# A diffusion layer in split fp32: the up projection by 512-column matmuls, with GpSimd off the weight splits

## The reference

```python
def conv_glu_ffn(h, w_up, conv_w, w_down, grid):
    up = h @ w_up                      # (256, 2048) @ (2048, 11264)
    up = dwconv2d_grid(up, conv_w)     # 3x3 taps per channel over a 4 x 64 grid
    a, b = jnp.split(up, 2, axis=-1)   # D_FF = 5632 each
    return (jax.nn.silu(a) * b) @ w_down
```

## Time and profile before

| | |
|---|---|
| Median of 3 runs | 2882.47 us |
| The profiled execution | 2887.08 us |
| Its span | 2884.3 us |
| TensorE busy | 2783.5 us (97%) |
| TensorE weight loads busy | 2101.3 us (73%) |
| VectorE busy | 1893.8 us (66%) |
| ScalarE busy | 991.5 us (34%) |
| GpSimd busy | 567.4 us (20%) |
| DMA | 412.84 MB, mean 143 GB/s |

### The profile page before, as it was taken

How to read it: one execution, slowest core, us unless ns; L and a number is a source line. 1 busy time by engine, 2 the same in 40 slices (tenths; PEclk the granted TensorE clock), 3 DMA queues, 4 the chain that set the end, 5 groups by cost and what they waited for, 6 DMA issues and landing times.

```text
span 2884.3 us, 66324 instructions
## 1 busy us (share of the span) xinstructions
PE 2783.5 (97%) x25890; PEld 2101.3 (73%) x25890; DVE 1893.8 (66%) x3509; ACT 991.5 (34%) x1684; POOL 567.4 (20%) x708
## 2 busy tenths in 40 slices
PE   5999999999999999999988999999899999999997
PEld 1456566666566666566655888887799999998886
DVE  2246677766677776667764656654589989995444
ACT  2232333322333322333312433333444444443332
POOL 0022332122333122233120200000023333330000
PEclk7999999999999999999989999999999999999999
DMA  9722122332222332222235455554445555554553
GB/s 388 284 91 97 55 89 96 111 111 96 63 86 89 111 111 96 77 79 89 75 121 195 141 183 188 189 189 165 170 141 180 186 178 187 177 185 154 186 180 139
DMA packets 75801, 412.84 MB, mean 143 GB/s; under 512 B 9296, under 2 KB 11984, under 8 KB 42608
## 3 DMA queue, kind: packets, MB, share of 16 engines
q1 hardware_dynamic: 74864, 408.10, 41.2%
q0 software_dynamic: 768, 2.10, 0.2%
HBM read 405.38 MB, written 4.19 MB: 142 GB/s over the span
## 4 chain that ended last, share of the span: by engine, by line
PE 91%; DVE 4%; DMA 2%; ACT 1%; issue 1%; SPq 0%; DVEq 0%; ACTq 0%; PEldq 0%
PE PB L723 21%; PE Q L992 13%; PE Q L987 7%; PE PB L987 4%; PE PB L982 4%; PE CH L987 3%; PE PB L983 3%; PE CH L983 3%; PE CH L982 3%; PE Q L859 3%; PE Q L845 3%; PE Q L866 2%; DMA ring<-w_mod_dram 2%; PE CH L900 2%; PE CH L930 1%; PE CH L920 1%
## 5 line engine op out<-in xcount | busy, mean ns | idle before, releaser
L723 PE MATMUL PB<-hT,ring 128*128 128x512 f32 (+1 forms) x1536 | 664.5, 550 | 1.5
L1721 DVE TENSOR_TENSOR w_lo_r<-ring,w_hi_r 128x1536 fp32r<-128x1536 f32 (+3 forms) x178 | 390.0, 2191 | 203.8 <-ACT w_hi_r L1307 203.8
L1307 ACT ACTIVATE w_hi_r<-ring 128x2048 fp32r<-128x2048 f32 (+2 forms) x178 | 325.8, 1830 | 313.6 <-PE PB L987 104.3
L723 PEld LDWEIGHTS PB<-hT,ring 128*128 128x128 f32 x1536 | 258.6, 189 | 126.3 <-issue 83.2
L1265 ACT ACTIVATE arena<-CH 128x64 f32<-128x64 f32 x128 | 28.6, 223 | 512.9 <-PE CH L903 324.3
L983 PE MATMUL PB<-hT_r,w_hi_r 128*128 128x256 f32 x832 | 204.7, 286 | 0.0
L1896 DVE TENSOR_TENSOR w_lo_r<-ring,w_hi_r 128x1408 fp32r<-128x1408 f32 x62 | 100.7, 1625 | 134.4 <-ACT w_hi_r L1426 134.4
L2007 POOL TENSOR_TENSOR w_lo_r<-ring,w_hi_r 128x512 fp32r<-128x512 f32 x88 | 118.1, 1342 | 357.1 <-ACT w_hi_r L1307 357.1
L1576 DVE SCALAR_TENSOR_TENSOR arena<-ring,csilp,arena 128x512 f32<-128x512 f32 x240 | 180.7, 753 | 5.9 <-DMA ring<-w_mod_dram 1.3
L992 PE MATMUL Q<-ff_r,w_hi_r 128*128 128x512 f32 x704 | 176.7, 399 | 3.5 <-ACT w_hi_r L1426 3.5
L982 PE MATMUL PB<-hT_r,w_hi_r 128*128 128x256 f32 x704 | 175.9, 289 | 2.8 <-DVE hT_r L1823 2.8
(11 more groups left out here) (268 smaller groups left out, 5337.0 us busy)
## 6 DMA issues: line engine op xcount, KB each, us to landing
ring<-w_up_dram SPq DMA_DIRECT2D x88, 1024.0 KB, 4.9
ring<-w_mod_dram SPq DMA_DIRECT2D x128, 512.0 KB, 3.7
ring<-w_rkv_dram SPq DMA_DIRECT2D x48, 1024.0 KB, 5.9
ring<-w_down_dram SPq DMA_DIRECT2D x64, 704.0 KB, 4.0
ring<-w_mod_dram SPq DMA_DIRECT2D x32, 1024.0 KB, 9.1
ring<-w_ga_dram SPq DMA_DIRECT2D x16, 1024.0 KB, 4.9
ring<-w_gb_dram SPq DMA_DIRECT2D x16, 1024.0 KB, 4.9
ring<-w_pa_dram SPq DMA_DIRECT2D x16, 1024.0 KB, 4.8
```

Of the source, the lines that this page charges most:

```text
L723: last = mm(PB[slot % 2][:, 0:cols], tile(n, kt), hT[:, kt, 0:cols], start=(kt == 0), stop=(kt == KT - 1))
L1307: f(w_hi_r[:, r % 2, 0:n], ring[:, r, 0:n], ACT.Copy).then_inc(hi_rdy, 1)
L1721: tt(w_lo_r[:, r, 0:n], ring[:, r, 0:n], as_f32(w_hi_r[:, r % 2, 0:n]), ALU.subtract).then_inc(lo_rdy, 1)
```

## The change

The up stage takes the form of the other stages. A high block is multiplied with low and high activations side by side in one matmul of 512 columns, which fills the whole bank, and the low weights go to the second half. ScalarE copies the first half of the bank into a new SBUF buffer `us[r]` (in the place of `woven`), VectorE adds the second half to it (`add_halves`), and only then does ScalarE make the centre tap, from `us`. The eight other taps read `us` too. The sum frees the bank (`up_sum`), so TensorE no longer waits for taps. GpSimd no longer splits weights: VectorE splits all 2048 columns. The product of silu and partner moves from VectorE to GpSimd, directly ahead of the split of its result. VectorE's order within a quad becomes: split, sums of tiles 0 and 1, last taps of the quad before, coefficient copy, split, first taps of pair 0, split, sums of tiles 2 and 3, last taps of pair 0, split, first taps of pair 1.

```diff
-POOL_COLS = 4 * P
+        us = [woven_sb[:, r].rearrange("p c t -> p (c t)")[:, 0:T] for r in range(4)]
 # TensorE, up_four
-                    pe.wait_ge(up_cv, i * 2 + 1 + r // 2)
+                    pe.wait_ge(up_sum, i * 4 + r + 1)
-                        with_high(four[r][:, 0:T], r, kt, h2_hi_r[:, kt], h2_lo_r[:, kt], kt == 0)
+                        mm(four[r][:, :], w_hi_r[:, r % 2, kt * P:(kt + 1) * P], hT_r[:, kt], start=(kt == 0), stop=False)
                     low_ready("up", i, r)
-                    pe.wait_ge(up_lo, i * 4 + r + 1)
-                        last = with_low(four[r][:, 0:T], r, kt, h2_hi_r[:, kt], kt == KT - 1)
+                        last = with_low(four[r][:, T:TT], r, kt, h2_hi_r[:, kt], kt == KT - 1)
 # ScalarE, up_four
                     product(r, "up", 0, i, 1)
                     if r % 2 == 0:
+                        act.wait_ge(up_cv, i * 2 + r // 2 + 1)
+                    f(us[r], four[r][:, 0:T], ACT.Copy).then_inc(up_half, 1)
+                    if r % 2:
                         act.wait_ge(ff_rdy, i * 2 + r // 2 + 1)
-                    f(cv[r], four[r][:, 0:T], ACT.Identity, scale=convw_a[:, r, 4:5]).then_inc(up_mid, 1)
+                        for q in (r - 1, r):
+                            act.wait_ge(up_sum, i * 4 + q + 5)
+                            f(cv[q], us[q], ACT.Identity, scale=convw_a[:, q, 4:5]).then_inc(up_mid, 1)
                     if r % 2:
                         highs("up", i, r, FT // 2, "down")
 # VectorE
-                r, n = r % 4, width(phase, r % 4) - (POOL_COLS if phase == "up" else 0)
+                r, n = r % 4, width(phase, r % 4)
-                        last = stt(grid(cv[r])[:, orow, ocol], grid(four[r][:, 0:T])[:, irow, icol],
+                        last = stt(grid(cv[r])[:, orow, ocol], grid(us[r])[:, irow, icol],
+            def add_halves(i, r):
+                dve.wait_ge(up_half, i * 4 + r + 1)
+                tt(us[r], us[r], four[r][:, T:TT], ALU.add).then_inc(up_sum, 1)
             def up_four(i, carry):
+                lows("up", i, 0, FT // 2, "down")
+                add_halves(i, 0)
+                add_halves(i, 1)
                 if carry is not None:
                     dve.wait_ge(dve_step, V.base)
                     taps(i - 1, 1, 1, carry)
-                lows("up", i, 0, FT // 2, "down")
-                if carry is not None:
                     dve.wait_ge(up_cv, i * 2 + 2)
                 V.need(V.tick(nc.vector.tensor_copy(convw_v, ...)))
+                lows("up", i, 1, FT // 2, "down")
                 prev = taps(i, 0, 0, [0, 0])
-                lows("up", i, 1, FT // 2, "down")
-                if carry is not None:
-                    gated(i - 1, 1)
+                lows("up", i, 2, FT // 2, "down")
+                add_halves(i, 2)
+                add_halves(i, 3)
                 taps(i, 0, 1, prev)
-                lows("up", i, 2, FT // 2, "down")
-                prev = taps(i, 1, 0, [0, 0])
                 lows("up", i, 3, FT // 2, "down")
-                gated(i, 0)
-                return prev
+                return taps(i, 1, 0, [0, 0])
 # GpSimd
-            def up_four(i, first):
-                for r in range(4):
-                    pool.wait_ge(hi_rdy, split_count("up", i, r))
-                    nc.gpsimd.tensor_tensor(w_lo_r[:, r, REG - POOL_COLS:], ring[...], as_f32(w_hi_r[...]), ALU.subtract)
-                    if r % 2 and not first:
-                        ff_split(i * 2 - 2 + r // 2)
+            def gated(i, j):
+                n = i * 2 + j
+                pool.wait_ge(up_act, i * 2 + j + 1)
+                nc.gpsimd.tensor_tensor(one(ff_lo, n), sil[j], cv[2 * j + 1], ALU.mult).then_inc(ff_rdy, 1)
+                split(ff_rdy, i * 2 + j + 3, ff_lo, ff_hi_r, ff_lo_r, n, i * 2 + j + (GG + KT + 1))
```

More of the change, by code:

```diff
@@ L337, in layer_kernel @@
         pool_lo = sem("activation_low_ready")
-        up_lo = sem("up_weight_low_ready")
         h2_raw = sem("h2_ready")
@@ L354, in layer_kernel @@
         xr_ld = sem("x_reloaded")
+        up_half = sem("up_low_activation_half_copied")
+        up_sum = sem("up_halves_added")
         up_mid = sem("up_centre_tap_done")
@@ L1083, in _ @@
             pe.sem_inc(up_cv, 2)
+            pe.sem_inc(up_sum, 4)
             pe.sem_inc(ff_rdy, 2)
@@ L1831, in taps @@
             def taps(i, j, half, prev):
-                if half == 0:
-                    dve.wait_ge(up_mid, i * 4 + 2 * j + 2)
                 for n in range(4 * half, 4 * half + 4):
@@ L1841, in taps @@
                         ocol, icol = slice(max(0, -b), GRID - max(0, b)), slice(max(0, b), GRID - max(0, -b))
-                        if n:
+                        if n == 0:
+                            dve.wait_ge(up_mid, i * 4 + r + 1)
+                        else:
                             V.need(prev[q])
                         w = 3 * (a + 1) + b + 1
-                        last = stt(grid(cv[r])[:, orow, ocol], grid(four[r][:, 0:T])[:, irow, icol],
+                        last = stt(grid(cv[r])[:, orow, ocol], grid(us[r])[:, irow, icol],
                                    convw_v[:, r, w:w + 1], grid(cv[r])[:, orow, ocol], ALU.mult, ALU.add)
@@ L1889, in _ @@
             taps(FT // 2 - 1, 1, 1, prev)
-            gated(FT // 2 - 1, 1)
             def low_down(i, k):
@@ L2000, in _ @@
                 split(m_rdy, i + 2, m_lo, m_hi_r, m_lo_r, i, i + (GG + 1))
-            def up_four(i, first):
-                for r in range(4):
-                    pool.wait_ge(hi_rdy, split_count("up", i, r))
-                    pool.sem_inc(seen, 1)
-                    nc.gpsimd.tensor_tensor(w_lo_r[:, r, REG - POOL_COLS:], ring[:, r, REG - POOL_COLS:],
-                                            as_f32(w_hi_r[:, r % 2, REG - POOL_COLS:]), ALU.subtract).then_inc(up_lo, 1)
-                    if r % 2 and not first:
-                        ff_split(i * 2 - 2 + r // 2)
[L2012 to L2019, removed]
+            def gated(i, j):
+                n = i * 2 + j
+                pool.wait_ge(up_act, i * 2 + j + 1)
+                pool.sem_inc(seen, 1)
+                nc.gpsimd.tensor_tensor(one(ff_lo, n), sil[j], cv[2 * j + 1], ALU.mult).then_inc(ff_rdy, 1)
+                split(ff_rdy, i * 2 + j + 3, ff_lo, ff_hi_r, ff_lo_r, n, i * 2 + j + (GG + KT + 1))
+            with pool.Fori(0, FT // 2) as i:
+                for j in range(2):
+                    gated(i, j)
 def tiles(w):
```

## The result

| | before | after |
|---|---|---|
| Median, same chip, 4 runs each | 2884.05 us (2879.65 to 2887.63) | 2906.70 us (2905.78 to 2907.08) |
| Ratio, 95% interval | | 1.0079 [1.0066, 1.0091] |
| The profiled execution, its span | 2887.08, 2884.3 | 2907.08, 2905.2 |
| One quad of the up stage | 23.04 us | 23.89 us |

The kernel is 0.8% slower, +22.7 us. The busy table of the stage comes first, in the columns of the earlier trace rows: the stretch, its length, then busy us of PE, PEld, DVE, ACT and POOL.

What follows compares the result with a forecast made beforehand. TensorE bounds at 23.04 us per quad; after the change VectorE would, at 21.44 + 2.75 = 24.2. Stage +23.2, start +0.55 and end +3.5 gave +27.2, taken as 2909 us, range 2898 to 2918.

Steps and rivals of the forecast that it cites:

- TensorE, 5.56 us per tile: Up stage: matmuls of 512 columns save 0.20 us per tile, making a TensorE-bound quad 22.24 us.
- VectorE without the port, 21.44: VectorE's us per up-stage quad before GpSimd collisions: splits 8.84, sums 1.32, taps 10.88, coefficient copy 0.40.
- The port, 2.75: Up stage: us per quad VectorE loses because it and GpSimd exclude each other reading SBUF, 1.37 per gating.
- GpSimd's product falls into the taps behind the split: Up stage: the gating product waits for VectorE's split, then falls with cast and subtraction into the next eight taps.
- The added waits: Up stage: centre taps waiting for sums hold VectorE 0 to 0.2 us per half quad, taken as nothing; bank-sum and DMA waits don't bind.
- The stage, +23.2: Up stage, tile 1 of quad 0 to that of quad 21: from 483.8 us to 507.0.
- Start +0.55 and end +3.5: Up stage's first sum starts 0.55 us later; last such sum to TensorE resuming in the down stage takes 26.3, not 22.8.
- The total, +27.2: Whole kernel: 2887.1 us of the profiled execution becomes 2914; from the median 2882.5 it is 2909.7.
- TensorE stays the bound: Rival: GpSimd's operations wait for VectorE or fall into idle time, quad 22.24 us, kernel 2868; chance 0.17.
- Taps from SBUF are cheaper: Rival: each up-stage tap 61 ns cheaper from SBUF, so TensorE bounds again, kernel 2868 us; chance 0.03.
- The port costs half: Rival: one of three GpSimd operations meets PSUM sums or a short wait, quad 22.85 us, kernel 2882; chance 0.12.
- the ScalarE chain: Rival: ScalarE's centre taps and splits add 0.3 us per half quad to VectorE, +12, kernel 2922; chance 0.08.

Runs made afterwards that it cites:

- e1: Changed kernel with the summed tile that the taps read placed in PSUM instead of SBUF; 2868.88 us, ratio 0.9941.
- e5: Changed kernel with GpSimd's product of each gating done twice, the first time into a spare tile; 2922.12 us, ratio 1.0138.
- e6: Changed kernel with the gated product back on VectorE, GpSimd only casting and subtracting; 2897.86 us, ratio 1.0050.
- e8: e1 with the high splits of down tiles 2 and 3 before the last silu, and the down stage accumulating in PB; 2868.73 us, ratio 0.9950.
- e4: Changed kernel with GpSimd's three operations per gating replaced by constant fills that read nothing; 2875.29 us, ratio 0.9967.

## Why the prediction was right, and where its sizes were off

The forecast was 2909 us, the result 2906.7. That they lie 2.3 us apart is in part luck: the forecast added 26.5 to a median of 2882.5, and measured were 22.7 on 2884.05. Its mechanism holds: VectorE becomes the bound, and it does so by the shared reading of SBUF. By its steps:

- **TensorE, 5.56 us per tile.** Right: the first tiles, before VectorE's backlog reaches them, follow each other by 5.56 (2108.36, 2113.93, 2119.49), and e1 runs at 22.27 per quad.
- **VectorE without the port, 21.44.** Measured 21.67: splits 8.81, sums 1.32, taps 4 x 2.75 = 11.00 for 10.88, the copy with its waits 0.54 for 0.40.
- **The port, 2.75.** Measured 2 x (3.86 - 2.75) = 2.22. This is the mis-sized term. Taken from splits and wide products, the price of a GpSimd operation of 0.74 was set at 0.58 and that of a cast at 0.20 (its own row gives 0.17); beside taps they cost 0.49, 0.15 and 0.48. e5 prices the product alone at 0.49, e6 at 0.48. The 2.22 lies just outside the 2.3 to 3.0 that the forecast's own range was built on; the time falls inside that range all the same, the term before it having come out 0.23 larger. The two errors (+0.23 and -0.53) partly cancel: 23.89 for 24.2. A port cost below 1.4 was named as the point where the kernel would gain; the 2.22 lies well above it, and with it at nothing (e1) the kernel does gain.
- **GpSimd's product falls into the taps behind the split.** Right: its row starts within the split and takes 2.08 or 2.62 for that reason.
- **The added waits.** Right that they bind nowhere: e1 keeps them, and its VectorE waits for no late centre tap. TensorE's gaps are VectorE's backlog handed on through the high split. They were expected at about 2 us per quad; the difference of the periods is 1.65 (23.89 less 22.24), and the busy table shows 0.98, as a matmul's shown duration is longer than its step.
- **The stage, +23.2.** Measured +17.1: 20 quads by 0.31 less are 6.2, which is all of the difference.
- **Start +0.55 and end +3.5.** Measured +1.1 and +3.0. At the end the 11 matmuls again take 4.98 us, at granted clock 0.50, which is the lower of the two levels (1.2 GHz), after 7.93 us without work; the tile behind them, 11 in 2.68, is at 1.00.
- **The total, +27.2.** +21.2 by the trace, +22.7 by the medians.

Of the rivals, "TensorE stays the bound" describes e1's quad, 22.27, but not the changed kernel; that e1's whole time is 2868.9 for the 2868 worked out is partly luck, as e1 has a wait of 4.0 us ahead of the down stage that this rival's sum did not have. "Taps from SBUF are cheaper" is refuted: without GpSimd beside them a tap of 189 or 192 columns starts 0.328 us after the one before it from SBUF and 0.322 to 0.325 from PSUM. "The port costs half" and the ScalarE chain did not come about.

Left open: why a stage begins at different times when nothing ahead of it was edited. The first sum stands at 2112.9 in the changed kernel and in e1, at 2110.2 in e8 and at 2106.9 in e5. In e5 the difference is older than the up stage: the first matmul of the merge stage already starts at 1646.22, in the changed kernel at 1652.70. It decided the miss of e5; no experiment was made on it. Medians that differ by less than some 6 us are therefore read here by their quads first.

## What to carry to other kernels

Before work moves between VectorE and GpSimd, ask of each VectorE operation how many of its inputs are in SBUF: the taps with one of them in PSUM ran beside GpSimd for nothing, those with two in SBUF paid for each GpSimd operation that reads SBUF, 0.15 us for a cast of 0.40 and 0.48 for a product of 0.74. Put the operand that many VectorE operations share into PSUM; here that one choice was worth 38 us, 33.5 of them within the stage, and turned a loss of 0.8% into a gain of 0.6%. And add up each engine's work per period, port price included, before a saving on the engine that bounds now is counted: it pays only down to the next engine's sum.

## What the runs showed of the hardware

- GpSimd's fills with a constant (256 columns, 0.31 us) neither wait for a VectorE split from two SBUF tensors nor stretch it; its product, which reads SBUF, waits it out (2.1 to 2.9 us).
- The same engine's long fills (two of 11264 columns, 18.97 us) let a VectorE split with two SBUF inputs run in its usual 2.29 us, but a VectorE copy of 36 columns from SBUF to SBUF took 9.59 us beside them, for 0.18 alone (e4).
- The exclusion costs both sides: beside SBUF taps GpSimd's cast takes 0.55 for 0.40 and its subtraction 0.87 for 0.74.
- The centre tap on ScalarE takes 0.50 us from SBUF and 0.47 from PSUM; VectorE's taps differ by under 0.01.
